# Mixture of experts in a two-layer decoder step: 64-row tiles in two weight lanes, ordered by expert size, with indirect weight loads

## The chip, the cores and the metric

The kernel runs as one program on one core of a Trainium2 chip. The metric is the device time of one execution in microseconds (us), lower is better. All data are float32.

## The reference

One inference step of a decoder with two layers (a gated linear attention layer, then a differential attention layer over a shared key and value cache). It takes a prompt of 512 tokens and 8 samples of one token each, 520 tokens in all, with a model width of 1024. Each layer ends with a mixture of experts: 16 experts in 4 groups, of which a token uses two of the same group.

```python
def moe_ffn(xm, w_router, b_router, w_gate, w_up, w_down):
    ...
    probs = jax.nn.softmax((xt @ w_router + b_router).astype(jnp.float32), axis=-1)
    pg = probs.reshape(-1, N_GROUPS, EXPERTS_PER_GROUP)
    gscore = jnp.sum(lax.top_k(pg, TOP_K)[0], axis=-1)
    gidx = jnp.argmax(gscore, axis=-1)
    in_group = jnp.take_along_axis(pg, gidx[:, None, None], axis=1)[:, 0]
    vals, idx = lax.top_k(in_group, TOP_K)
    wts = vals / jnp.sum(vals, axis=-1, keepdims=True)
    ...
    for e in range(N_EXPERTS):
        h = jax.nn.silu(xt @ w_gate[e]) * (xt @ w_up[e])
        y = y + comb[:, e:e + 1] * (h @ w_down[e])
    return y.reshape(shp)
```

`w_gate` and `w_up` of an expert are 1024 x 512, `w_down` is 512 x 1024: three matrices of 2 MB. 520 tokens with two experts each make 1040 rows per layer. How many rows an expert gets depends on the data. For the inputs of this case it is, for experts 0 to 15:

- layer 0: 32, 28, 30, 38, 43, 145, 110, 114, 117, 40, 82, 59, 54, 23, 86, 39
- layer 1: 130, 106, 126, 6, 153, 160, 5, 9, 18, 9, 68, 43, 101, 4, 8, 93

## The kernel before

The program is a row of stages with a barrier of all engines between them: the conditioning vectors, the projections of the first layer (`stage_gla_project`), its attention (`stage_gla`), the output projection and norm, then `stage_route`, `stage_experts` and `stage_combine` for the mixture of experts, then the second layer's attention (`stage_decoder`) and again route, experts and combine.

`stage_route` (L1223) multiplies the rows by the router's matrix, picks two experts per token on VectorE (DVE), counts with TensorE (PE) how many rows each expert has and which rank a row has within its expert (`rk_mm`), and from that computes with a chain of small DVE operations (L1348, L1425 to L1504): the slot of each row (`dest`), the row of each slot (`idx`), the expert of each tile (`texp`), whether a tile has more than 64 rows (`full`), and the number of pairs of tiles. Meanwhile SP loads the weights of tiles 0 and 1.

`stage_experts` (L1507) works on tiles of 128 rows. Tile n is expert n for the first 16; tiles behind them take what an expert has above 128 rows; one expert may be split in halves so that the number of tiles is even. Layer 0 has 18 tiles, layer 1 has 20. The loop `tiles` runs every engine through the tiles in order, and tiles alternate between two sets of buffers, u = 0 and 1. For tile n:

- POOL copies a column of `idx` (L1560) and gathers up to 128 rows of x by an indirect DMA (L1563), after the x transposes of an earlier tile.
- PE transposes x (L1577, 8 instructions), ACT copies the transposes (L1653), PE computes gate and up (L1629): 16 matmuls of 512 columns in two column tiles of 64 (the trace counts 32 instructions) for the first 64 rows. If `full` says so, a branch (L1593, its value loaded at L1599) does the same for the second 64 rows.
- ACT applies silu (L1675, L1676), DVE multiplies by up (L1706).
- PE transposes h (L1586, 4), ACT copies it (L1659), PE computes down (L1611, 16 instructions for 64 rows, 32 for 128), DVE and ACT copy y (L1699, L1664, L1665), and ACT's queue stores 512 KB of y (L1668).
- SP loads gate and up for tile n once the gate/up product of tile n-2 has freed the buffer, and down of tile n-1 once the down product of tile n-3 has (`load_expert`, L1204; the DMAs are L1210). The expert's number is read into a register, and every tile loads its three matrices, 2 MB each.

On PE the order for tile n is: gate/up of n, h transposes of n-1, x transposes of n+1, down of n-1. `stage_combine` (L1713) gathers two rows of y per token (L1760) and adds them by their weights. Rows of the y store that no tile reaches are filled with finite values once: `stage_gla` does that with one DMA of 4 MB on SP (L898), behind its loads of the recurrent state (L592). `stage_gla_project` (L340) runs before it; the last things that SP issues there are loads at L192 and L380.

Of the kernel before, what the change touches and what calls it, by code (L numbers as in the profile page):

```python
# [8 lines left out]
I32 = mybir.dt.int32  # L9
# [5 lines left out]
P = 128  # L15
# [52 lines left out]
def allocate(nc, ctx):  # L68
# [26 lines left out]
    m.psd = lambda n: m.ps[n]  # L95
    m.modD = nc.dram_tensor("mod_rows", (NVEC, NS + 1, D), F32).ap()
# [243 lines left out]
def stage_gla_project(nc, ctx, m, a, ahead):  # L340
# [5 lines left out]
    sh_mm, sh_cp, sm_mm, sm_ev = (sem(n) for n in ("sh_mm", "sh_cp", "sm_mm", "sm_ev"))  # L346
# [21 lines left out]
    with nc.Block() as block:  # L368
        @block.sync
        def _(sp):  # L370
            ada_next = {2: range(0, 5), 3: range(5, 9), 4: range(9, 13), 5: range(13, 16)}
            for c in range(1, 6):
# [8 lines left out]
                if c == 1:  # L381
# [7 lines left out]
                    sp.dma_start(gn, a["gn_a"][0].partition_broadcast(P)).then_inc(gn_in, 16)  # L389

# [204 lines left out]
def stage_gla(nc, ctx, m, a, states, w_out):  # L595
# [6 lines left out]
    y_fill, eg_ok, q_zero, qk_zero, qs_ok, kr_mm, kr_ok, ks_ok, kv_mm, st_ok, so_mm, o_out = (sem(n) for n in  # L602
        ("y_fill", "eg_ok", "q_zero", "qk_zero", "qs_ok", "kr_mm", "kr_ok", "ks_ok", "kv_mm", "st_ok", "so_mm", "o_out"))
# [34 lines left out]
    with nc.Block() as block:  # L638
# [254 lines left out]
        def _(sp):  # L893

            most = 2 * MIN_PAIRS * P
            for n in range(NS // 2):
                states.load(sp, n)
            sp.dma_start(m.yD[most:SLOTS, :].rearrange("(t p) n -> p t n", p=P),  # L898
                         m.x[:, 0:1, :].to_broadcast([P, (SLOTS - most) // P, D])).then_inc(y_fill, 16)

# [15 lines left out]
            sp.wait_ge(y_fill, 16)  # L916
# [280 lines left out]
def expert_weights(nc, ctx, m, l, a):  # L1197

    return [(n, [view(m.W, (2 * j + u) * 4096, k, 4096 // k) for u in range(2)], a[f"w_exp_{n}"][l],
             [ctx.enter_context(m_semaphore(nc, f"moe{l}_{n}_in{u}")) for u in range(2)], k)  # L1200
            for j, (n, k) in enumerate((("gate", KT), ("up", KT), ("down", FF // P)))]


def load_expert(sp, m, weights, tile, u, free=None):  # L1204

    e = tile if isinstance(tile, int) else sp.value_load(m.texp[0:1, tile], min_val=0, max_val=NE - 1)
    for name, buf, source, loaded, k in weights:
        if free is not None:
            wait(sp, *free[name])
        sp.dma_start(buf[u].rearrange("p k n -> p (k n)"),  # L1210
                     source[bass.ds(e, 1)].rearrange("a (p k) n -> p (a k n)", k=k)).then_inc(loaded[u], 16)
# [11 lines left out]
def stage_route(nc, ctx, m, l, a, weights, router, ada=None):  # L1223
# [19 lines left out]
    half_of, pick, room, odd = (take(1, NE)[:, 0, :] for _ in range(4))  # L1243
    over, steps = take(NE, NTT - 1), take(1, NTT - 1)[:, 0, :]
# [5 lines left out]
    nt, start, end, zero16 = (take(1, NE)[:, 0, :] for _ in range(4))  # L1250
    tmp16 = take(1, NE)[:, 0, :]
    lim = take(1, NE)[:, 0, :]
    cmp_ = take(SLOT_TILES, NE)
    cmp2 = take(MORE, NE)
    first, far = take(1, NE)[:, 0, :], take(NTT, NE)
    tix, tef = take(1, SLOT_TILES)[:, 0, :], take(1, SLOT_TILES)[:, 0, :]

    NJ = 2 * NTT
    tok, tile0, row0 = take(1, NTT)[:, 0, :], take(1, SLOT_TILES + 1)[:, 0, :], take(1, P)[:, 0, :]
    slot, row = take(2, NTT), take(1, NJ)[:, 0, :]  # L1260
    reached, token_at, row_hot = take(NJ, SLOT_TILES + 1), take(NJ, SLOT_TILES), take(NJ, P)
    assert off[0] <= 9 * D
    with nc.Block() as block:
        @block.sync
        def _(sp):
            sp.dma_start(m.lnr[:, 0, :], a["ln_ffn_g"][l].partition_broadcast(P)).then_inc(ln_in, 16)
            sp.dma_start(m.lnr[:, 1, :], a["ln_ffn_b"][l].partition_broadcast(P)).then_inc(ln_in, 16)
            load_expert(sp, m, weights[0:1], 0, 0)
            load_expert(sp, m, weights[0:1], 1, 1)
            if ada is not None:  # L1270
                sp.wait_ge(ada.used, Ada.STEPS)
            load_expert(sp, m, weights[1:3], 0, 0)
            load_expert(sp, m, weights[1:2], 1, 1)
            sp.wait_ge(ln_in, 32)

        @block.gpsimd
        def _(g):
# [10 lines left out]
            nc.gpsimd.iota(first, pattern=[[P, NE]], base=0, channel_multiplier=0, allow_small_or_imprecise_dtypes=True).then_inc(tab, 1)  # L1288
            nc.gpsimd.iota(tix, pattern=[[1, SLOT_TILES]], base=0, channel_multiplier=0,
                           allow_small_or_imprecise_dtypes=True).then_inc(tab, 1)  # L1290
            nc.gpsimd.iota(tok, pattern=[[P, NTT]], base=0, channel_multiplier=1, allow_small_or_imprecise_dtypes=True).then_inc(tab, 1)
            nc.gpsimd.iota(tile0, pattern=[[P, SLOT_TILES + 1]], base=0, channel_multiplier=0,
                           allow_small_or_imprecise_dtypes=True).then_inc(tab, 1)
            nc.gpsimd.iota(row0, pattern=[[1, P]], base=-P, channel_multiplier=0, allow_small_or_imprecise_dtypes=True).then_inc(tab, 1)
            nc.gpsimd.iota(steps, pattern=[[P, NTT - 1]], base=P, channel_multiplier=0, allow_small_or_imprecise_dtypes=True).then_inc(tab, 1)
# [5 lines left out]
        def _(pe):  # L1301
# [42 lines left out]
        def _(v):  # L1344
# [15 lines left out]
            V.memset(zero16, 1.0)  # L1360
# [31 lines left out]
            def first_of(onehot, score, best, weights, n):  # L1392
# [30 lines left out]
            tt(over, m.ps[5][:, 0:NE].unsqueeze(2).to_broadcast([P, NE, NTT - 1]), steps.unsqueeze(1).to_broadcast([P, NE, NTT - 1]),  # L1423
               ALU.is_gt)
            V.tensor_reduce(out=nt, in_=over, axis=AX.X, op=ALU.add)  # L1425
            V.scalar_tensor_tensor(out=half_of, in0=m.ps[5][:, 0:NE], scalar=0.5 * P, in1=over[:, :, 0], op0=ALU.is_gt, op1=ALU.subtract)
            v.drain()
            V.tensor_tensor_scan(end, zero16, nt, 0.0, ALU.mult, ALU.add)
            v.drain()
            V.tensor_scalar(odd[:, 1:1 + MORE // 2], tix[:, 1:MORE:2], end[:, NE - 1:NE], None, ALU.is_equal)  # L1430
            V.tensor_tensor_scan(room, zero16, half_of, 0.0, ALU.mult, ALU.add)
            v.drain()
            V.tensor_reduce(out=odd[:, 0:1], in_=odd[:, 1:1 + MORE // 2], axis=AX.X, op=ALU.add)
            V.scalar_tensor_tensor(out=pick, in0=room, scalar=1.0, in1=half_of, op0=ALU.is_equal, op1=ALU.mult)
            v.drain()
            V.tensor_scalar(pick, pick, odd[:, 0:1], None, ALU.mult)
            v.drain()
            tt(nt, nt, pick, ALU.add)
            V.tensor_tensor_scan(end, zero16, nt, 0.0, ALU.mult, ALU.add)
            V.tensor_scalar(room, pick, -0.5 * P, float(P), ALU.mult, ALU.add)  # L1440
            v.drain()
            tt(start, end, nt, ALU.subtract)

            V.tensor_tensor(far, m.ps[3][:, 0:NTT * NE].rearrange("p (i e) -> p i e", e=NE),
                            room.unsqueeze(1).to_broadcast([P, NTT, NE]), ALU.is_ge)
            V.scalar_tensor_tensor(out=lim, in0=start, scalar=float(P), in1=first, op0=ALU.mult, op1=ALU.subtract)
            v.drain()
            V.tensor_tensor(lim, lim, room, ALU.subtract)
            v.drain()
            V.tensor_scalar(lim, lim, float(NE * P), None, ALU.add)  # L1450
            V.tensor_tensor(RK, m.ps[3][:, 0:NTT * NE].rearrange("p (i e) -> p i e", e=NE),
                            first.unsqueeze(1).to_broadcast([P, NTT, NE]), ALU.add)
            v.drain()
            tt(far, far, lim.unsqueeze(1).to_broadcast([P, NTT, NE]), ALU.mult)
            tt(RK, RK, far, ALU.add)

# [1193 lines left out]
```

## Time and profile before

| | |
|---|---|
| three executions, median (lowest to highest) | 1887.97 us (1885.96 to 1888.25) |
| span of the profiled execution | 1878.7 us |
| what the median has more than that span | 9.3 us |
| PE busy / share of the span | 1551.5 us / 83% |
| DVE, ACT, POOL busy | 679.1, 404.9, 352.2 us |
| DMA | 551.63 MB, mean 294 GB/s |

The span is the time between the first and the last instruction that the profiler recorded. The profiled execution has no time of its own besides it; the difference to the median of the plain executions is what lies around the span (and what profiling itself does). Engines are PE (TensorE), PEld (its weight loads), DVE (VectorE), ACT (ScalarE), POOL (GpSimd) and SP (SyncE, which only issues DMAs here); "q" behind a name means that engine's queue or sequencer. A line such as L1629 is a line of the kernel. A stage is read from its own window, since a share over the whole span mixes stages with different limits.

### The profile page before, as it was taken

The numbers are of one execution on the slowest core, as the hardware profiler recorded it, in microseconds if no ns is written. First come the engines' busy times: TensorE is split into PE (matmuls) and PEld (weight loads), VectorE is DVE, ScalarE is ACT, GpSimd is POOL, SyncE is SP. The second block draws the span as 40 slices with busy tenths as digits, with TensorE's granted clock in tenths as the row PEclk, the third lists the DMA queues.
The fourth block names the chain that finished last, engine by engine and source line by source line (L and its number), as shares of the span: only waits on it lengthen the run. The fifth ranks groups of instructions, "written<-read, shape, count | busy, mean of one in ns | idle before, by whom it ended". The sixth has DMA issues, their size and how long they took to land. (4 is left out here: it accounts for less than half of the span.)

```text
span 1878.7 us, 21805 instructions
## 1 busy us (share of the span) xinstructions
PE 1551.5 (83%) x7246; PEld 676.2 (36%) x7247; DVE 679.1 (36%) x1228; ACT 404.9 (22%) x914; POOL 352.2 (19%) x277
## 2 busy tenths in 40 slices
PE   5999996597689998956999987887495599989965
PEld 2333344443333333313443334444142233333321
DVE  1001118475300000046945448886175300000006
ACT  1001015221121212212121113444321021222220
POOL 0000001000100000021745469872000100000001
PEclk8999997698799999977999998889697699999996
DMA  8564605726699999796889999997504499999963
GB/s 320 199 269 163 271 2 190 240 109 240 251 425 426 392 378 417 319 344 230 310 297 364 398 353 409 367 351 302 197 23 154 168 425 381 418 419 398 429 263 134
DMA packets 119419, 551.63 MB, mean 294 GB/s; under 512 B 16453, under 2 KB 37814, under 8 KB 97307
## 3 DMA queue, kind: packets, MB, share of 16 engines
q1 hardware_dynamic: 94962, 492.46, 66.4%
q10 hardware_dynamic: 15424, 37.28, 5.4%
q0 software_dynamic: 8944, 20.76, 3.2%
q8 instruction: 49, 0.80, 0.2%
q14 instruction: 40, 0.33, 0.0%
HBM read 521.82 MB, written 40.03 MB: 299 GB/s over the span
## 5 line engine op out<-in xcount | busy, mean ns | idle before, releaser
L1629 PE MATMUL ps<-arena_w,arena_r 128*64 128x512 f32 x1600 | 364.4, 612 | 27.1 <-issue 22.2
L1629 PEld LDWEIGHTS ps<-arena_w,arena_r 128*64 128x64 f32 x1600 | 121.1, 141 | 263.6 <-issue 257.4
L1611 PE MATMUL ps<-arena_w,arena_r 128*64 128x512 f32 x800 | 183.4, 606 | 19.2 <-ACT arena_r L1659 19.2
L1706 DVE TENSOR_TENSOR arena_r<-arena_r,ps 128x512 f32<-128x512 f32 x38 | 26.2, 688 | 419.9 <-ACT arena_r L1676 419.9
L2036 POOL TENSOR_TENSOR arena_w<-arena_w,arena_r 128x1024 f32<-128x1024 f32 x55 | 129.5, 2360 | 84.7 <-DMA arena_w<-in_cache_k_dram 84.3
L2036 POOL TENSOR_TENSOR arena_r<-arena_r 128x1024 f32<-128x1024 f32 x56 | 134.0, 2398 | 44.5 <-DMA arena_r<-in_cache_k_dram 44.3
L2089 PE MATMUL ps<-arena_w,xt 128*128 128x512 f32 x256 | 114.9, 606 | 1.3 <-ACT xt L2265 1.3
L450 PE MATMUL ps<-arena_w,xt 128*128 128x512 f32 x256 | 113.0, 597 | 1.0 <-DVE arena_w L533 0.6
L1098 PE MATMUL ps<-arena_w,xt 128*128 128x512 f32 x256 | 111.4, 593 | 0.0
L1560 POOL COPY small<-idx 128x1 int32 (+1 forms) x38 | 7.0, 183 | 510.4 <-PE ps L1577 459.3
L1611 PEld LDWEIGHTS ps<-arena_w,arena_r 128*64 128x64 f32 x800 | 55.3, 139 | 121.0 <-issue 99.2
L1675 ACT ACTIVATE arena_r<-ps 64x512 f32<-64x512 f32 x38 | 22.4, 588 | 339.2 <-PE ps L1629 339.2
L1699 DVE COPY arena_r<-ps 128x512 f32<-128x512 f32 x38 | 26.3, 692 | 188.5 <-PE ps L1611 188.5
L2431 DVE TENSOR_REDUCE arena_r<-arena_w 128x16 f32<-128x1024 f32 x64 | 76.1, 1212 | 36.0 <-POOL arena_w L2036 36.0
L2431 DVE TENSOR_REDUCE arena_r<-arena_r 128x16 f32<-128x1024 f32 x64 | 76.0, 1211 | 15.0 <-POOL arena_r L2036 14.8
L1739 PE MATMUL ps<-arena_r,xt 128*128 128x512 f32 (+1 forms) x80 | 46.6, 740 | 41.8 <-DMA arena_r<-y_rows,dest 30.2
L450 PEld LDWEIGHTS ps<-arena_w,xt 128*128 128x128 f32 x256 | 47.6, 190 | 65.7 <-issue 64.9
L2104 PE MATMUL ps<-arena_m,arena_r 128*16 128x512 f32 x480 | 64.6, 660 | 7.7 <-DMA arena_m<-in_cache_v_dram 7.7
L2089 PEld LDWEIGHTS ps<-arena_w,xt 128*128 128x128 f32 x256 | 48.7, 194 | 59.8 <-issue 58.2
L1098 PEld LDWEIGHTS ps<-arena_w,xt 128*128 128x128 f32 x256 | 48.0, 190 | 59.1 <-issue 59.1
L415 PE MATMUL ps<-xt,arena_w 128*128 128x512 f32 x128 | 59.7, 621 | 4.0 <-PEq L249 3.7
L1278 POOL MEMSET arena_r<- 128x128 f32 x2 | 0.4, 204 | 304.3 <-POOLq L951 304.3
(393 smaller groups left out, 1941.9 us busy)
## 6 DMA issues: line engine op xcount, KB each, us to landing
arena_w<-in_w_exp_gate_dram SPq DMA_DIRECT2D x38, 2048.0 KB, 13.7
arena_w<-in_w_exp_up_dram SPq DMA_DIRECT2D x38, 2048.0 KB, 17.3
arena_w<-in_w_exp_down_dram SPq DMA_DIRECT2D x38, 2048.0 KB, 16.7
arena_m<-in_cache_v_dram SPq DMA_DIRECT2D x120, 512.0 KB, 7.1
arena_w<-in_cache_k_dram SPq DMA_DIRECT2D x64, 512.0 KB, 8.2
arena_r<-in_cache_k_dram SPq DMA_DIRECT2D x64, 512.0 KB, 7.0
arena_w<-in_w_ada_dram SPq DMA_DIRECT2D x12, 2048.0 KB, 14.5
arena_m<-in_w_ada_dram SPq DMA_DIRECT2D x12, 2048.0 KB, 9.2
```

The source lines that it names most:

```text
L415: last = nc.tensor.matmul(m.ps[n % 2][:, :], w, m.xt[:, k, 0:SEQ], start=(k == 0), stop=(k == KT - 1))
L450: last = nc.tensor.matmul(m.ps[4 + n % 4][:, :], m.xt[:, k, i * P:(i + 1) * P], m.wr[c % 2][:, k, :], start=(k == 0), stop=(k == KT - 1))
L1098: last = nc.tensor.matmul(m.ps[(4 if n % 2 else 6) + c][0:r, :], m.xt[:, k, i * P:i * P + r], w.of(k, c), start=(k == 0), stop=(k == KT - 1))
L1611: last = nc.tensor.matmul(psy[c][at:at + 64, :], ht[u][:, k, 64 * (1 - a):64 * (2 - a)], wd[u][:, k, c * 512:(c + 1) * 512], start=(k == 0 ...
L1629: last = nc.tensor.matmul(ps[at:at + 64, :], xgt[u][:, k, 64 * a:64 * (a + 1)], w[u][:, k, :], start=(k == 0), stop=(k == KT - 1), tile_po ...
L1699: V.tensor_copy(ys[u][:, 0:512], psy[0][:, :]).then_inc(y_v, 1)
L1706: V.tensor_tensor(hs[u], es[u], psu[:, :], ALU.mult).then_inc(h_ok, 1)
L1739: last = nc.tensor.matmul(y_ps[i % 2][n][0:r, :], dg[c][i][0:r, 0:r], y[i % 2][c][0:r, n * 512:(n + 1) * 512], start=(c == 0), stop=(c == 1))
L2036: G.tensor_tensor(kp[n % RING], kp[n % RING], qb[b % 2], ALU.mult).then_inc(pp_ok, 1)
L2089: last = nc.tensor.matmul(bank[:, :], m.xt[:, k, i * P:(i + 1) * P], dec.both[c % 4 // 2][:, k, :], start=(k == 0), stop=(k == KT - 1))
L2104: last = nc.tensor.matmul(PSO[n][32 * g:32 * g + C, :], PR[b % 2][:, GRP * q + g, :], value_at(GRP * v + g)[:, n * 512:(n + 1) * 512], sta ...
L2431: V.tensor_reduce(out=S[b % 2][:, j, :], in_=kp[n % RING].rearrange("p (c d) -> p c d", d=DHB), axis=AX.X, op=ALU.add).then_inc(ks_ok, 1)
```

## The change

The mixture of experts is organized anew.

- **Tiles** have 64 rows (`TR`). Two of them, one in lane 0 (rows 0 to 63 of a pair) and one in lane 1 (rows 64 to 127), make a pair; each lane has one buffer for each of the three matrices. The pair shares one gather of x, one set of x transposes, one of h transposes.
- **Order.** The experts are ranked by their number of rows on the chip (a 16 x 16 comparison). Expert 0 is forced to the head of lane 0, expert 1 to that of lane 1. Even ranks go to lane 0 in falling order, odd ranks to lane 1 in rising order. The tiles of an expert follow each other in its lane. For the rows above that makes 12 pairs in layer 0 and 14 in layer 1. The lanes (expert: rows of its tiles):
  - layer 0, lane 0: 0: 32; 8: 64, 53; 6: 64, 46; 10: 64, 18; 12: 54; 9: 40; 3: 38; 13: 23; one empty tile. Lane 1: 1: 28; 2: 30; 15: 39; 4: 43; 11: 59; 14: 64, 22; 7: 64, 50; 5: 64, 64, 17.
  - layer 1, lane 0: 0: 64, 64, 2; 4: 64, 64, 25; 12: 64, 37; 10: 64, 4; 8: 18; 7: 9; 3: 6; 13: 4. Lane 1: 1: 64, 42; 6: 5; 14: 8; 9: 9; 11: 43; 15: 64, 29; 2: 64, 62; 5: 64, 64, 32; one empty tile.
- **Weights** of later tiles are loaded by POOL with indirect DMAs of 128 rows of 16 KB. The row numbers are computed on the chip; where a tile continues the expert of the tile before it, they lie out of bounds and the DMA moves nothing. Only the first tile of each lane is loaded by SP, at the end of the route stage.
- **Short arm.** A value per tile chooses between two code arms for each product: above 32 rows two column tiles of 64 rows with 512 columns, otherwise four column tiles of 32 with 256 columns each (gate/up; the moving operand takes 2 of every 4 columns) or with half of the sum each (down), and DVE adds the two halves (`y_join`).
- **Order of PE** for pair i: gate/up of lane 0, down of pair i-1 in lane 0, gate/up of lane 1, x transposes of pair i+1, down of pair i-1 in lane 1, h transposes of pair i.
- **Stores of y**: 64 rows as two DMAs of 512 columns per tile, on SP, behind ACT's copy and `y_join`.
- **Ahead of the loop** POOL makes three index tables, and DVE computes from them which tiles take which arm (`full_ok`) and which rows each load takes (`col_ok`): about eight operations on 128 x 832 or 128 x 52 elements. PE waits for `full_ok` ahead of the first product.
- **Routing**: the DVE chain in `stage_route` has other operations, for ranks, lanes and starts.
- **The y fill** grows to 8 MB and moves from `stage_gla` to the end of SP's program in `stage_gla_project`, with a wait for it there.

```diff
-    return [(n, [view(m.W, (2 * j + u) * 4096, k, 4096 // k) for u in range(2)], a[f"w_exp_{n}"][l],
...
+             a[f"w_exp_{n}"].rearrange("l e (p k) n -> (l e p) (k n)", k=k))
...
@@ stage_gla_project, sync engine @@
+            least = MIN_PAIRS * P
+            sp.dma_start(m.yD[least:SLOTS, :].rearrange("(t p) n -> p t n", p=P),
+                         m.x[:, 0:1, :].to_broadcast([P, (SLOTS - least) // P, D])).then_inc(y_fill, 16)
+            sp.wait_ge(y_fill, 16)
...
@@ stage_route, vector engine, behind the counts @@
+            V.scalar_tensor_tensor(out=key, in0=count, scalar=float(NE), in1=bias, op0=ALU.mult, op1=ALU.add)
...
+            V.tensor_tensor(larger, along(key), across(key), ALU.is_gt)
...
+            V.tensor_reduce(out=rank_of, in_=larger, axis=AX.X, op=ALU.add)
...
+            V.scalar_tensor_tensor(out=key, in0=lane, scalar=-100.0, in1=rank_of, op0=ALU.mult, op1=ALU.add)
...
@@ stage_experts, gpsimd @@
+            def load(which, nexts, at, i, u):
+                nc.gpsimd.tensor_copy(at[u], col[:, bass.ds(i + u * COLS, 1)])
+                g.drain()
+                for (_, buf, _, _, _, rows), landed in zip(which, nexts):
+                    g.indirect_dma_start(out=buf[u].rearrange("p k n -> p (k n)"), out_offset=None, in_=rows,
+                                         in_offset=bass.IndirectOffsetOnAxis(ap=at[u], axis=0),
+                                         bounds_check=DEPTH * NE * P - 1, oob_is_err=False).then_inc(landed[u], 16)
+
+            def step(i, t):
+                g.wait_ge(gu_mm, 2 * i + 1)
+                load(weights[0:2], (wg_next, wu_next), gi, i + 1, 0)
+                if t != 0:
+                    g.wait_ge(d_mm, 2 * i - 1)
+                    load(weights[2:3], (wd_next,), di, i, 0)
+                g.wait_ge(x_tr, i + 2)
+                gather(i + 2)
+                g.wait_ge(gu_mm, 2 * i + 2)
+                load(weights[0:2], (wg_next, wu_next), gi, i + 1, 1)
+                if t != 0:
+                    g.wait_ge(d_mm, 2 * i)
+                    load(weights[2:3], (wd_next,), di, i, 1)
...
@@ stage_experts, tensor engine @@
+            def by_size(i, u, done, whole, half):
+
+                full = pe.value_load(m.full[0:1, bass.ds(i + u * COLS, 1)], min_val=0, max_val=1)
                 with pe.If_ne(full.val, 0):
-                    product(1).then_inc(done, 1)
+                    whole().then_inc(done, 1)
                 with pe.Else():
-                    pe.nop().then_inc(done, 1)
+                    half().then_inc(done, 1)
...
+                def half():
+                    for k in range(KT):
+                        for j in range(4):
+                            w = (wg, wu)[j // 2][u][:, k, :].rearrange("p (a b) -> p a b", b=FT)
+                            out = psg[u][QR * j:QR * (j + 1), :].rearrange("t (a b) -> t a b", b=FT)
+                            last = nc.tensor.matmul(out[:, :, 0:2], xgt[:, k, TR * u:TR * u + QR], w[:, :, j % 2 * 2:j % 2 * 2 + 2],
+                                                    start=(k == 0), stop=(k == KT - 1), tile_position=(0, QR * j))
...
+            def step(i, t):
+                gate_up(i, 0, t == 0)
                 if t != 0:
...
+                    down(i - 1, 0, t == 1)
+                gate_up(i, 1, t == 0)
+                x_transpose(i + 1, False)
                 if t != 0:
...
+                    down(i - 1, 1, t == 1)
+                h_transpose(i, t == 0)
+
             pe.wait_ge(zeroed, 1)
...
+            x_transpose(0, True)
+            pe.wait_ge(full_ok, 1)
+            pairs = loop(pe, step)
...
@@ stage_experts, vector engine @@
+            def y_join(i, u):
+                V.tensor_copy(sf[u], small[:, bass.ds(i + u * COLS, 1)])
+                v.drain()
+                v.wait_ge(y_s, 2 * i + u + 1)
+                for c in range(2):
+                    r, over = slice(TR * c, TR * c + QR), slice(TR * c + QR, TR * (c + 1))
+                    last = V.scalar_tensor_tensor(out=ys[u][r, :], in0=psy[u][over, :], scalar=sf[u][over, :], in1=ys[u][r, :],
+                                                  op0=ALU.mult, op1=ALU.add)
+                last.then_inc(y_v, 1)
...
+            V.tensor_tensor(begun, at, each(code), ALU.is_ge)
+            V.tensor_tensor(within, at, each(full_to), ALU.is_lt)
+            v.drain()
+            V.tensor_tensor(begun, begun, within, ALU.mult)
...
+            v.drain().then_inc(full_ok, 1)
```

## Rows read from the trace of the kernel before

**Rows 1.** Busy windows, expert stages: span, engines (PE to POOL), PEclk, DMA share, GB/s.

```profile
486.00:804.00 318.00, 282.98 (x1320) 109.61 (x1320) 26.31 (x40) 71.79 (x128) 21.75 (x36) 0.95 0.89 367
...
1475.00:1829.00 354.00, 322.66 (x1536) 123.67 (x1536) 28.88 (x44) 79.74 (x142) 23.83 (x39) 0.97 0.89 368
```

**Rows 2.** The waits: engine line waited for: total us, times, longest.

```profile
ACT arena_r L1675 <- PE ps L1629: 339.2, 38, 19.8
```

**Rows 3.** The waits of SP's DMA queue, same columns.

```profile
SPq L1210 <- PE ps L1629: 323.9, 34, 24.2
```

**Rows 4.** PE in time: start, length (us), line, operands, idle before.

```profile
711.47 7.04 PE L1629 MATMUL ps<-arena_w,arena_r 128*64 128x512 f32 x32
718.44 0.75 PE L1586 MATMUL ps<-ident,arena_r 128*128 128x128 f32 x4
719.02 1.06 PE L1577 MATMUL ps<-ident,arena_r 128*128 128x128 f32 x8
720.41 3.65 PE L1611 MATMUL ps<-arena_w,arena_r 128*64 128x512 f32 x16 [0.32 <-ACT arena_r L1659]
728.07 16.49 PE L1629 MATMUL ps<-arena_w,arena_r 128*64 128x512 f32 x64 [4.00 <-issue]
```

**Rows 5.** Busy windows at the late product of the group above.

```profile
726.40:733.20 6.80, 5.13 (x12) 1.64 (x14) 0.00 (x0) 0.00 (x0) 0.00 (x0) 0.50 1.01 424
733.20:790.00 56.80, 54.41 (x268) 20.93 (x266) 4.83 (x7) 13.48 (x24) 1.20 (x2) 1.00 0.94 383
```

**Rows 6.** The costliest groups: out<-in xcount | busy, mean ns | idle before.

```profile
L1629 PE MATMUL ps<-arena_w,arena_r 128*64 128x512 f32 x1600 | 364.4, 612 | 27.1 <-issue 22.2
```

**Rows 7.** PE in order of time, in the first layer's attention.

```profile
314.94 3.63 PE L865 MATMUL ps<-arena_m,arena_w 128*8 128x256 f32 x64
```

**Rows 8.** POOL in order of time: one gather of x.

```profile
544.64 0.18 POOL L1560 COPY small<-idx 128x1 int32 x1 [13.79 <-PE ps L1577]
545.72 1.01 POOL L1563 DMA_INDIRECT arena_r<-xm_rows,small  x1 [0.90 <-issue]
```

**Rows 9.** Line L1563, the x gathers: ns min/median/max, landing.

```profile
L1563 POOL DMA_INDIRECT arena_r<-xm_rows,small x38: 1004/1014/1239, 487.2 to 1767.7; - x38
...
DMA to landing us min/median/max: 3.4/10.9/12.6
```

**Rows 10.** Line L1760, the gathers of y rows.

```profile
L1760 POOL DMA_INDIRECT arena_r<-y_rows,dest x20: 852/942/1950, 804.5 to 1855.2; - x20
```

**Rows 11.** Line L1599, the value load on PE's queue.

```profile
L1599 PEldq FUSED_REGOPS  x110: 37/151/156, 492.3 to 1813.2; - x110
L1599 PEldq TENSOR_LOAD <-full x76: 297/303/695, 491.9 to 1812.9; - x76
```

**Rows 12.** Line L1593, the branch on PE's queue.

```profile
L1593 PEldq COMPARE_BRANCH  x100: 66/200/352, 498.5 to 1818.9; - x100
```

**Rows 13.** PE in order of time: the first product of layer 0.

```profile
493.99 8.91 PE L1629 MATMUL ps<-arena_w,arena_r 128*64 128x512 f32 x32 [1.16 <-ACT arena_r L1653]
```

**Rows 14.** The costliest groups again: a DVE copy of 512 columns.

```profile
L1699 DVE COPY arena_r<-ps 128x512 f32<-128x512 f32 x38 | 26.3, 692 | 188.5 <-PE ps L1611 188.5
```

**Rows 15.** DVE in order of time: the first instruction of combine.

```profile
803.88 0.06 DVE L1766 MEMSET small<- 128x1 f32 x1 [3.95 <-PEq L1543]
```

**Rows 16.** DVE in order of time, route of layer 1: chain's ends.

```profile
1460.16 0.23 DVE L1348 TENSOR_TENSOR arena_r<-ps,arena_r 128x64 f32<-128x64 f32 x1 [1.55 <-PE ps L1324]
...
1466.03 0.41 DVE L1348 TENSOR_TENSOR arena_r<-arena_r 128x250 f32<-128x250 f32 x1
```

**Rows 17.** SP in order of time, from the projection stage's end.

```profile
217.30 0.55 SPq L380 DMA_DIRECT2D arena_w<-in_w_in_a_dram  x1
284.28 6.07 SPq L592 DMA_DIRECT2D arena_m<-in_state_gla_dram  x4
```

**Rows 18.** DMA issues: out<-in xcount, KB each, median us to landing.

```profile
y_rows<-x_res SPq DMA_DIRECT2D x1, 4096.0 KB, 19.7
```

**Rows 19.** DMA queues: packets, MB, share of 16 engines.

```profile
q0 software_dynamic: 8944, 20.76, 3.2%
```

More of the change, by code:

```diff
@@ L1441, in _ @@
+            V.tensor_reduce(out=tiles[:, 1:2], in_=start, axis=AX.X, op=ALU.add)
+            V.tensor_reduce(out=both_lanes, in_=nt, axis=AX.X, op=ALU.add)
+            V.tensor_reduce(out=passed, in_=whole, axis=AX.X, op=ALU.add)
             v.drain()
[L1442 to L1446, printed above, removed]
+            V.tensor_tensor(larger, along(key), across(key), ALU.is_lt)
@@ L1526, in stage_experts @@
[L1526 to L1540 removed]
+    FT, HW = FF // P, FF // 2
@@ L1640, in _, with x_copy @@
             pe.wait_ge(zeroed, 1)
-            x_transpose(0, 0, True)
-            pairs = tiles(pe, step)
-            full = is_full(bass.ds(2 * pairs - 1, 1))
-            h_transpose(1, 2 * pairs - 1)
-            down(1, 2 * pairs - 1, 16 * pairs, full)
+            x_transpose(0, True)
+            pe.wait_ge(full_ok, 1)
+            pairs = loop(pe, step)
+            for u in range(2):
+                down(pairs - 1, u, False)
         @block.scalar
         def _(s):
-            def x_copy(u, n):
-                s.wait_ge(x_tr, n + 1)
-                wait(s, gu_mm, 2 * n - 2)
+            def x_copy(i, first):
+                s.wait_ge(x_tr, i + 1)
+                if not first:
+                    s.wait_ge(gu_mm, 2 * i)
@@ L1688, in _ @@
+                h_copy(i, t == 0)
+            x_copy(0, True)
+            pairs = loop(s, step)
+            for u in range(2):
+                y_keep(pairs - 1, u, False)
         @block.vector
@@ new lines, in _ @@
+            V.tensor_tensor(within, at, each(code), ALU.is_equal)
+            v.drain()
+            V.tensor_copy(m.full[0:1, :], fullf[0:1, :])
+            V.tensor_scalar(small, fullf, -1.0, 1.0, ALU.mult, ALU.add)
+            V.tensor_tensor(within, within, each(ew), ALU.mult)
+            v.drain().then_inc(full_ok, 1)
+            V.tensor_reduce(out=lanes(fullf), in_=within, axis=AX.X, op=ALU.add)
+            v.drain()
+            V.tensor_scalar(col, fullf, prow, None, ALU.add).then_inc(col_ok, 1)
@@ L1713, in stage_combine @@
+            pairs = loop(v, step)
+            for u in range(2):
+                y_join(pairs - 1, u)
 def stage_combine(nc, ctx, m, l, a, stores=None, ada_groups=(), vectors=(), dec=None):
```

452 lines of the change are left out of this document (236 added, 216 removed).

## The prediction

> **What bounds the kernel now.** I read the stages first (the busy windows), then the waits, then TensorE's own order in time. The two expert stages are the two windows of [rows 1]: 318.0 and 354.0 us, with PE busy for 282.98 and 322.66 us, so the array works for nine tenths of them; the DMA engines are 0.89 busy at the same time and carry 367 GB/s, that is 412 GB/s when all are busy. One expert is 6.29 MB, 15.2 us of that wire: 10.2 for gate and up, 5.1 for down. ACT's longest wait is for the gate/up product [rows 2], and the loads on SP wait for the same product [rows 3]: a buffer comes free late, then the wire runs. So array and wire take turns at being last. TensorE's order [rows 4] gives the prices of the array: gate/up of 64 rows 7.04 us (6.9 to the next start), of 128 rows twice that, 13.9, down of 64 rows 3.65 (3.5 net), h transposes 0.6, x transposes 1.0, 0.3 of gap ahead of a down product. The last row there shows what a late load costs: 4.00 us of idle, then 16.49 us where 13.9 is normal. In those first 6.80 us the granted clock was 0.50 (1.2 GHz), behind them 1.00 (2.4 GHz) [rows 5]; the excess is 2.6.
>
> **The work after.** The router of the reference, worked through for its own inputs, gives the rows of each expert; 38 tiles and 50 products of 64 rows (1600 instructions of 32 each, [rows 6]) follow from it for the kernel before, as the trace has them. After: layer 0 has 12 pairs (16 tiles above 32 rows, 8 of 32 or fewer), layer 1 has 14 pairs (15 and 13). Both load 14 experts on the way, where 16 and 18 tile loads stood. In each layer one tile of the short ones is empty. Of the 11 steps from pair to pair in layer 0, 5 bring new weights to both lanes, 4 to one, 2 to none; of 13 in layer 1, 4, 6 and 3.
>
> **Prices not in the trace.** The short gate/up arm is 64 matmuls four wide over 256 columns. The nearest row is the 3.63 us of 64 such matmuls, 57 ns each [rows 7]; ends 3.5 (half of 7.04) and 7.0 (nothing won). I take 3.6, and 1.75 for the short down product. An expert load by indirect DMA: the x gather takes 0.18 for its copy, 0.90 to the issue, 1.01 for the issue [rows 8]; it lands after 3.4 at best [rows 9], of which 1.3 is wire. So a load costs 1.1 + 2.1 + wire. Rows four times as long are not in the trace; between 8 rows and 128 the issue hardly differs (0.852 to 0.942, at most 1.950, [rows 10]), so I take 1.01, with 0.85 and 4 times 1.01 as ends. A value load and branch behind a late wait cost 0.30 + 0.15 + 0.20 = 0.65, with their gaps 0.8 [rows 11, 12]; ends 0 and 1.0.
>
> **One step.** Array: gate/up and down of both lanes, transposes: 6.9 + 3.5 + 6.9 + 1.0 + 3.5 + 0.6 = 22.4 with full tiles. Lane 0 new: its load starts after its gate/up product and needs 1.1 + 2.1 + 10.2 + 0.8 = 14.2; 15.5 of array lie beside it, so it is hidden while that cover is full; with short tiles it is not. Lane 1 new: POOL has the x gather ahead of the load in its queue, and that waits for the x transposes: 1.0 + 2.4 + 14.2 = 17.6 against 15.5, so 2.1 is exposed: 24.5 with a full product, 21.2 with a short one. Both new: the wire is continuous, 1.1 + 2.1 + 10.2 + 5.1 + 10.2 + 0.8 = 29.5 from one gate/up end in lane 0 to the lane 1 product, less the 3.5 of the down product between: 26.0. x gather and y stores (0.5 MB each per pair) share that wire: 2.5 more, 28.5 (ends 26.0 and 30.5). POOL takes its waits in order (lane 0's gate/up, its down, the x gather, lane 1's gate/up, its down), so a late down product of lane 0 would hold the gather, and that lane 1's load; on the array it comes ahead of lane 1's gate/up product and the x transposes, which end 6.9 + 1.0 later, so it holds nothing. Lane 1's down weights then hold the wire for 8.6 us of the next step; if that step loads lane 0, it lands 5.4 later.
>
> Going through the pairs by these prices: layer 0, both new 5 x 28.5 = 142.5; one new 24.5 + 24.5 in lane 1, and in lane 0 behind a step with both new 14.2 + 5.4 and a full or a short product, 26.5 + 23.2, together 98.7; none 2 x 19.1 (3.5 + 6.9 + 1.0 + 3.5 + 0.6 and a short product of 3.6) = 38.2. Layer 1: both new 4 x 28.5 = 114; one new 21.2 + 21.2 + 24.5 in lane 1, 23.2 and twice 14.2 + 3.6 = 17.8 in lane 0, together 125.7; none 15.4 (first step, no down products yet), 20.7 and 17.4 (with one and three short products), together 53.5.
>
> **Head, tail, clock.** The first product starts 8.0 us after the stage begins [rows 13]; it now waits for some six DVE operations on 128 x 832 elements, about 1.0 each from 0.692 for 512 [rows 14], of which 2.8 stick out: 10.8. The first product itself comes off idle, 8.91 instead of 7.04 [rows 13], so 8.9 in layer 1 and 5.4 for the short one in layer 0. Tail: the rest of the last pair, 14.2 and 12.5; then the store and the block's end, 4.6 today (DVE's last copy, 0.69, and 3.95 of idle ahead of combine at 803.88, [rows 14, 15]), plus 1.6 for joining two halves (a small copy, ACT's copy and two DVE operations in line where two engines copied side by side): 6.2. Late loads let the clock fall: 7 and 5 waits of 4 us or more, 1.8 each (the excess of 2.6 above for a product twice as long, 8.91 against 7.04 for one), half of it beside the next load: 6.3 and 4.5 (ends 0 and 31 for both).
> Layer 0: 10.8 + 5.4 + 142.5 + 98.7 + 38.2 + 20.4 + 6.3 = 322.3, today 318.0: +4.3. Layer 1: 10.8 + 8.9 + 114 + 125.7 + 53.5 + 18.7 + 4.5 = 336.1, today 354.0: -17.9.
>
> **The other edits.** Routing: the chain from the ranks' product to the row of slots is 5.87 us of DVE now [rows 16]; about 27 operations of 0.17 to 0.41 in its place give 8.9, less 0.6 on the shorter tail behind it: +2.4 per layer, +4.8 (ends 0 and 10). The y fill doubles to 8 MB and moves to SP's last place in the projection stage: SP issues its last load there at 217.30 and has nothing until the next stage's at 284.28 [rows 17]; the 4 MB fill took 19.7 us to land [rows 18], so 8 MB take 39 at most beside products that end the stage, with 28 us to spare. If that cover went, 39 would be the worst. Taken from the state loads' stage, where it is issued behind them and waited for last, it frees nothing. y stores move from ACT to SP, which has nothing else left to do: nothing. Weight loads leave SP for POOL: counted above. Three index tables are made on POOL behind the first gather and beside its landing of 3.4 us [rows 9], and the second gather, which they delay, is needed a product later: nothing, at most the 2.8 of the head again. Two arms for every product make PE's code longer; no wait of the trace is put down to its fetching: nothing, at worst one branch of 0.65 a step, 16.
>
> Sum: +4.3 - 17.9 + 4.8 = -8.8 on the profiled execution's span of 1878.7 us. The median of the three runs, 1887.97, is 9.3 above that span; I take those 9.3 as unchanged: 1869.9 + 9.3, **1879**.
>
> **Rivals.** (a) *More is hidden*: x and y slip into gaps of the wire (9 x 2.5 = 22), no clock loss (11), no lane-1 wait (5 x 2.1 = 10): about 1836. For it: the wire has a tenth free [rows 1]; against it: one buffer per lane, so every load waits for a product. (b) *Costs cancel*, 1884 to 1892: the steps with both new at 29 to 30 (nine of them, 0.5 to 1.5 more each): the wire never catches up. (c) *POOL becomes the bound, the other side*: seven indirect DMAs and five copies a step, some 14 us by [rows 8] today, in order, with waits between. Each new lane has two issues on its chain; 19 steps load. At 1.2 us an issue the gain is gone, at 2.0 it is 19 x 2 x 1.0 = 38: 1917. For it: rows of 16 KB not seen yet, one issue of 1.95 [rows 10]; against it: 1004 to 1239 ns in 38 gathers [rows 9]. (d) *Strided moving operands don't stream at the price of* [rows 7]: 21 short tiles x 3.3 = 69 us of array, half on the path: 1914. (e) *The skip doesn't skip*: every step loads both lanes, 15 further loads and more, above 1950; against it the software queue's 20.76 MB [rows 19]: 38 gathers of 128 rows and 20 of y would be 30 MB, the valid rows of both are 17.
>
> By the Trainium skill (DMA: Bandwidth & Descriptors, SWDGE vs HWDGE vs iDMA) descriptor rings are SBUF state that GpSimd writes and that DVE's 2-port mode locks it out of, so issues would stretch beside DVE work; an estimate from 26.31 us of DVE in the stage [rows 1], twice that after, is 0.2 us an issue, 8 us, and the sum 1887. The gathers' 1239 ns at most [rows 9] shows hardly any of it.
> The Trainium skill (TensorE: Matmul & The Clock Gate, "Wait — 56ns, not 53.3ns?") gives about 62 ns of sequencer per matmul when hardware decode is off, 3.97 us for 64 of them; [rows 7] shows 57 ns, 3.63 us. By the page the sum would be 21 x 0.34 = 7 us of array more, half of it on the path.
>
> **Chances.** Forecast 0.40 (own range 1850 to 1884); (a) 0.12; (b) 0.16; (c) 0.21; (d) 0.09; (e) 0.02. Faster by over 0.2% (3.8 us, about what a measurement of this kernel can tell) 0.52, same 0.16, slower 0.32. The range takes (a) in at 1836 and (c), (d) up to 1915: 1835 to 1915.
>
> **What would show it.** Right: stages near 322 and 336 us; both-new steps at 28 to 29 us; short products at 3.6; POOL issues near 1.0; first product about 11 us in. Wrong: issues of 1.3 us or more on POOL, or steps without loads above 23 us, or short products of 5 and more; then (c) or (d) decides. Stages below 300 would mean (a).

## The result, and the profile after

The changed kernel takes 2291.27 us (median of 4; 2282.11 to 2298.47) where the kernel before takes 1888.11 us: a ratio of 1.212, 95% interval 1.208 to 1.217. It is 403 us slower; the forecast was 9 us faster, with 1915 as the upper end of the range.

The busy windows by stage show where. Columns are as in [rows 1]; the second and the fourth line are the expert stages.

```profile
0.00:491.00 491.00, 395.33 (x1848) 184.16 (x1849) 169.59 (x370) 86.15 (x170) 10.67 (x35) 0.89 0.56 213
491.00:997.60 506.60, 283.43 (x1560) 108.67 (x1560) 65.69 (x112) 50.43 (x87) 96.82 (x147) 0.78 0.55 199
997.60:1684.50 686.90, 540.05 (x2502) 257.99 (x2502) 426.33 (x721) 161.86 (x460) 286.25 (x160) 0.84 0.77 288
1684.50:2245.00 560.50, 317.25 (x1938) 121.75 (x1938) 75.16 (x127) 58.45 (x101) 112.79 (x171) 0.76 0.50 182
```

506.6 and 560.5 us stand against 318.0 and 354.0 in [rows 1]: 395 of the 417 us by which the two profiled executions differ (spans of 2296.0 and 1878.7). PE is busy about as long as before although the stage is far longer, its clock has fallen to 0.78 and 0.76, and the DMA engines, 0.89 busy before, stand at 0.55 and 0.50. So neither the array nor the wire is last. The waits name the engine (total us, times, longest):

```profile
DVE arena_r L1761 <- ACT arena_r L1725: 688.7, 52, 24.2
POOL arena_w L1578 <- issue: 626.7, 147, 13.8
ACT arena_r L1725 <- PE ps L1654: 501.9, 31, 25.1
PEld ps L1654 <- issue: 423.3, 465, 18.0
...
PE ps L1654 <- issue: 250.6, 24, 17.2
...
POOL arena_r L1571 <- issue: 132.7, 28, 10.7
```

POOL stands idle for 626.7 us ahead of its indirect weight loads (L1578) and for 132.7 us ahead of the x gathers (L1571), and no other engine releases it ("issue"). In order of time on POOL, in layer 0, the lane 1 half of one step of the loop and the lane 0 half of the next:

```profile
561.59 0.19 POOL L1575 COPY small<-xt 128x1 int32<-128x1 int32 x1
565.78 1.01 POOL L1578 DMA_INDIRECT arena_w<-in_w_exp_gate_dram,small  x1 [4.00 <-issue]
567.10 0.99 POOL L1578 DMA_INDIRECT arena_w<-in_w_exp_up_dram,small  x1 [0.31 <-issue]
568.10 0.20 POOL L1575 COPY small<-xt 128x1 int32<-128x1 int32 x1
580.84 1.01 POOL L1578 DMA_INDIRECT arena_w<-in_w_exp_down_dram,small  x1 [12.55 <-issue]
581.87 0.19 POOL L1575 COPY small<-xt 128x1 int32 x1
590.80 1.01 POOL L1578 DMA_INDIRECT arena_w<-in_w_exp_gate_dram,small  x1 [8.75 <-issue]
592.12 0.99 POOL L1578 DMA_INDIRECT arena_w<-in_w_exp_up_dram,small  x1 [0.30 <-issue]
593.12 0.19 POOL L1575 COPY small<-xt 128x1 int32 x1
606.23 1.01 POOL L1578 DMA_INDIRECT arena_w<-in_w_exp_down_dram,small  x1 [12.91 <-issue]
```

Each DMA issue takes 1.0 us, as the x gathers did [rows 8]. The copies of the indices start at once, so the semaphores that POOL waits on have come long before. But behind each copy the next DMA starts late: 4.00 us behind an x gather, 8.75 behind 2 MB, 12.55 and 12.91 behind 4 MB issued just before; the second DMA of a pair (up behind gate), which has no copy between, follows after 0.30. Between copy and DMA stands one instruction that the trace has no row for: `g.drain()`. [rows 8] shows the same place with 0.90.

What the drain waits for can be read from the landings. The view of DMAs, asked for the first six DMAs above one by one (the last number is us from issue to landing):

```profile
arena_r<-xm_rows,small POOLq DMA_INDIRECT x1, 4.4
arena_w<-in_w_exp_gate_dram,small POOLq DMA_INDIRECT x1, 8.8
arena_w<-in_w_exp_up_dram,small POOLq DMA_INDIRECT x1, 12.8
arena_w<-in_w_exp_down_dram,small POOLq DMA_INDIRECT x1, 9.1
arena_w<-in_w_exp_gate_dram,small POOLq DMA_INDIRECT x1, 9.0
arena_w<-in_w_exp_up_dram,small POOLq DMA_INDIRECT x1, 13.2
```

So the x gather landed at 564.97, and the next DMA starts 0.81 us later; up landed at 579.90 (0.94), down at 589.94 (0.86), the second up at 605.32 (0.91). The drains of both stages stand in 130 such places. In 121 of them an earlier DMA of POOL's was still on its way when the copy was done, and the DMA behind the drain starts 0.79 to 1.20 us behind the last landing; in the other 9 nothing was, and it starts 0.89 to 1.00 us behind the copy.

### The profile page after: what moved, and what is told of

The parts are those of the page before. It is cut to its first block and busy times, and to the rows that moved or that the text cites. A ratio compares the mean times of both kernels' runs of the same rounds, so it can differ in the third digit from the quotient of the medians.

```text
span 2296.0 us, 23818 instructions
## 1 busy us (share of the span) xinstructions
PE 1561.4 (68%) x7886; PEld 681.2 (30%) x7887; DVE 769.7 (34%) x1374; ACT 362.5 (16%) x834; POOL 517.7 (23%) x523
## 3 DMA queue, kind: packets, MB, share of 16 engines
q0 software_dynamic: 29680, 196.96, 23.2%
## 5 line engine op out<-in xcount | busy, mean ns | idle before, releaser
L1654 PE MATMUL ps<-arena_w,arena_r 128*64 128x512 f32 x992 | 268.7, 703 | 253.5 <-issue 250.6
L1761 DVE TENSOR_TENSOR arena_r<-arena_r,ps 64x512 f32<-64x512 f32 x52 | 35.9, 690 | 688.7 <-ACT arena_r L1725 688.7
L1654 PEld LDWEIGHTS ps<-arena_w,arena_r 128*64 128x64 f32 x992 | 89.2, 162 | 423.5 <-issue 423.3
L1663 PE MATMUL ps<-arena_w,arena_r 128*32 128x256 f32 x1344 | 109.5, 494 | 107.3 <-issue 105.2
L1769 DVE SCALAR_TENSOR_TENSOR arena_r<-ps,small,arena_r 32x512 f32<-32x512 f32 x104 | 78.0, 750 | 224.9 <-ACT arena_r L1731 224.2
L1725 ACT ACTIVATE arena_r<-ps 64x512 f32<-64x512 f32 x52 | 30.6, 588 | 705.1 <-PE ps L1654 501.9
L1680 PE MATMUL ps<-arena_w,arena_r 128*64 128x512 f32 x496 | 122.8, 641 | 26.5 <-issue 17.3
L1578 POOL DMA_INDIRECT arena_w<-in_w_exp_down_dram,small x48 | 48.7, 1015 | 375.9 <-issue 374.1
L1578 POOL DMA_INDIRECT arena_w<-in_w_exp_gate_dram,small x52 | 52.8, 1015 | 238.0 <-issue 238.0
L1663 PEld LDWEIGHTS ps<-arena_w,arena_r 128*32 128x32 f32 x1344 | 50.7, 137 | 168.9 <-issue 153.2
L1688 PE MATMUL ps<-arena_w,arena_r 128*32 128x512 f32 x336 | 52.2, 744 | 47.1 <-issue 45.2
L457 PEld LDWEIGHTS ps<-arena_w,xt 128*128 128x128 f32 x256 | 47.9, 191 | 66.0 <-issue 65.2
```

The costliest lines, as they stand in the source:

```text
L457: last = nc.tensor.matmul(m.ps[4 + n % 4][:, :], m.xt[:, k, i * P:(i + 1) * P], m.wr[c % 2][:, k, :], start=(k == 0), stop=(k == KT - 1))
L1578: g.indirect_dma_start(out=buf[u].rearrange("p k n -> p (k n)"), out_offset=None, in_=rows, in_offset=bass.IndirectOffsetOnAxis(ap=at[u], ...
L1654: last = nc.tensor.matmul(psg[u][TR * j:TR * (j + 1), :], xgt[:, k, lane_rows[u]], w[u][:, k, :], start=(k == 0), stop=(k == KT - 1), tile ...
L1663: last = nc.tensor.matmul(out[:, :, 0:2], xgt[:, k, TR * u:TR * u + QR], w[:, :, j % 2 * 2:j % 2 * 2 + 2], start=(k == 0), stop=(k == KT - ...
L1680: last = nc.tensor.matmul(psy[u][TR * c:TR * (c + 1), :], ht[:, k, lane_rows[u]], wd[u][:, k, c * 512:(c + 1) * 512], start=(k == 0), stop ...
L1688: last = nc.tensor.matmul(psy[u][QR * j:QR * (j + 1), :], ht[:, b, TR * u + QR * s:TR * u + QR * (s + 1)], wd[u][:, 2 * s + b, c * 512:(c ...
```

## The experiments

**Without the drain.** The drain only has to keep the DMA from reading an index that the copy has not written yet. A semaphore does that too (the small addition carries the wait):

```diff
-                nc.gpsimd.tensor_copy(at[u], col[:, bass.ds(i + u * COLS, 1)])
-                g.drain()
+                nc.gpsimd.tensor_copy(at[u], col[:, bass.ds(i + u * COLS, 1)]).then_inc(ready[u], 1)
+                g.wait_ge(ready[u], i)
+                nc.gpsimd.tensor_tensor(spare, code[:, 0:1], code[:, 0:1], ALU.add)
```

and the same in `gather`. Expected:

> The drain that POOL executes between copying an index column and issuing the indirect DMA is replaced by a semaphore that the copy raises. Theory D (the drain waits until every DMA that POOL issued earlier has landed, so its loads run one pair at a time and also wait for the skipped ones): idle time of POOL ahead of its indirect weight loads falls from 626.7 us to below 150, the two expert stages from 507 and 560 us to 320 to 350 each, the whole to 1880 to 1930 us. Rival Q (the software queue has room for two 2 MB loads only, and a third issue waits for room): the 12 to 13 us of idle behind each pair of gate and up loads stay, the whole stays above 2200. Rival W (indirect loads are slow on the wire itself): POOL's idle time goes but the product's wait on PE stays, landing grows beyond 25 us in the median, the whole stays above 2150.

Measured: 1932.44 us, ratio to the kernel before 1.023 (1.018 to 1.028). 359 of the 403 us are gone, though the total lies just above the 1930 that D allowed, and the second stage above its 350. POOL's idle time ahead of its loads falls from 626.7 to 69.0 us. On POOL the loads now follow each other, each 0.53 us after its addition:

```profile
545.38 0.20 POOL L1578 COPY small<-xt 128x1 int32<-128x1 int32 x1
545.67 0.19 POOL L1580 TENSOR_TENSOR small<-xt 128x1 f32<-128x1 f32 x1
546.38 1.03 POOL L1582 DMA_INDIRECT arena_w<-in_w_exp_gate_dram,small  x1 [0.53 <-issue]
547.72 0.99 POOL L1582 DMA_INDIRECT arena_w<-in_w_exp_up_dram,small  x1 [0.30 <-issue]
548.72 0.19 POOL L1578 COPY small<-xt 128x1 int32<-128x1 int32 x1
549.00 0.19 POOL L1580 TENSOR_TENSOR small<-xt 128x1 f32<-128x1 f32 x1
549.71 1.03 POOL L1582 DMA_INDIRECT arena_w<-in_w_exp_down_dram,small  x1 [0.53 <-issue]
```

These are lane 1's gate and up for pair 2 (expert 15) and its down for pair 1 (expert 2), all new: three loads of 2 MB issued within 4.4 us. The queue has room for more than two, and rival Q is out. W is out as well: it wanted landings of over 25 us in the median, and they take 10.7 (22.7 at most); the stages are 330.9 and 379.0 us (first index copy on POOL to the first instruction of combine), at 305 and 269 GB/s. The loads are the changed kernel's own; only the wait between them went.

**The drain back at one place.** In e1_no_drain the drain stands again ahead of the x gather, and only there:

```diff
-                nc.gpsimd.tensor_copy(xi, m.idx[:, bass.ds(i, 1)]).then_inc(xi_ok, 1)
-                g.wait_ge(xi_ok, i + 1)
-                nc.gpsimd.tensor_tensor(spare, code[:, 0:1], code[:, 0:1], ALU.add)
+                nc.gpsimd.tensor_copy(xi, m.idx[:, bass.ds(i, 1)])
+                g.drain()
```

> As e1_no_drain, but with the drain back ahead of the x gather alone, one of five in a step. Theory D (a drain lasts until POOL's earlier DMAs have landed): the idle time ahead of the gather is 5 us and more in the steps in which lane 0 got new weights just before, 2.5 or less in the others; lane 1's load starts that much later; the whole is 50 to 130 us above e1_no_drain. Rival F (a drain costs a fixed time, whatever is under way): the same idle time in every step, and about a fifth of the 359 us between the changed kernel and e1_no_drain, 70 us. Idle times tell the two apart.

Measured: 2006.91 us, ratio 1.063 (1.058 to 1.068), 74 us above e1_no_drain. That total fits both theories; the idle times of the gathers (last column) fit only one:

```profile
522.74 1.02 POOL L1573 DMA_INDIRECT arena_r<-xm_rows,small  x1 [10.85 <-issue]
...
550.70 1.02 POOL L1573 DMA_INDIRECT arena_r<-xm_rows,small  x1 [1.33 <-issue]
...
584.51 1.02 POOL L1573 DMA_INDIRECT arena_r<-xm_rows,small  x1 [6.27 <-issue]
...
613.85 1.01 POOL L1573 DMA_INDIRECT arena_r<-xm_rows,small  x1 [1.44 <-issue]
```

These are the gathers of the first four steps. Lane 0 changes its expert in the steps to pairs 1 and 3 and keeps it in those to 2 and 4; the drain waits 10.85 and 6.27 us in the former, 1.33 and 1.44 in the latter. So it is not a fixed price. But the change of lane 0 alone doesn't tell its length: of the 14 steps of both layers with new weights in lane 0, six stay under the 5 us expected (2.74 to 4.85), and of the 12 others three exceed 2.5 (3.16, 6.09 and 7.04). The landings do. In 17 of these 26 steps a landing later than the copy is on record, and the gather starts 1.07 to 1.17 us behind it; in eight every landing on record lies before the end of the copy, and the wait is 1.10 to 1.44 (in the two shown, a down matrix of 2 MB landed at 546.51 and 612.09, ahead of copies at 549.19 and 612.24). The landing that the first one, 10.85, waited for is not in the view. That is theory D: the drain lasts until the DMAs that POOL issued before have landed.

**The same drain in the kernel before.** The replacement at the one gather per tile of the kernel before:

```diff
-                nc.gpsimd.tensor_copy(ixc[u], m.idx[:, bass.ds(2 * i + u, 1)])
-                g.drain()
+                nc.gpsimd.tensor_copy(ixc[u], m.idx[:, bass.ds(2 * i + u, 1)]).then_inc(ix_ok, 1)
+                g.wait_ge(ix_ok, 2 * i + u + 1)
+                nc.gpsimd.tensor_tensor(spare, m.wts[:, 0, 0:1], m.wts[:, 0, 0:1], ALU.add)
```

> The kernel before with the same replacement of the drain ahead of its x gather. Theory D: its gathers (512 KB, one a tile, 12 us and more apart) have mostly landed when the next drain comes, so the drain cost nothing there: within 0.3% of the kernel before, the idle time ahead of the gathers falls from 51 to 20 to 30 us. Rival F: some 1 us a tile that lies on no path: the same time too, so the time alone can't tell them; what would speak against both is a gain of more than 0.5%.

Measured: 1892.51 us, ratio 1.002 (1.000 to 1.004). The idle time ahead of the gathers (L1563, L1564 here) falls from 51.3 to 19.4 us, and the time doesn't fall. A drain that waits for one gather, with a product's time to spare, was hidden there. That it waits could have been read from the kernel before, at the head of its first expert stage, in the same view as [rows 8]:

```profile
487.24 1.24 POOL L1563 DMA_INDIRECT arena_r<-xm_rows,small  x1 [0.98 <-issue]
488.50 0.19 POOL L1560 COPY small<-idx 128x1 int32<-128x1 int32 x1
491.62 1.02 POOL L1563 DMA_INDIRECT arena_r<-xm_rows,small  x1 [2.93 <-issue]
```

The second gather's copy is done at 488.69, and the DMA starts 2.93 later instead of 0.90 to 0.98: the first gather, issued at 487.24, was still on its way (PE starts on it at 490.88).

**The order on POOL.** From e1_no_drain, the x gather is moved behind lane 1's gate and up loads:

```diff
-                g.wait_ge(x_tr, i + 2)
-                gather(i + 2)
                 g.wait_ge(gu_mm, 2 * i + 2)
                 load(weights[0:2], (wg_next, wu_next), gi, gi_ok, i + 1, 1)
+                g.wait_ge(x_tr, i + 2)
+                gather(i + 2)
```

> As e1_no_drain, and the x gather is moved on POOL behind lane 1's gate and up loads. Theory D with the prediction's step prices: lane 1's load starts up to 2.4 us plus the x transposes earlier wherever lane 1 is new, in 9 + 5 steps; 10 to 30 us below e1_no_drain. If the loads' own issue or the wire is last in those steps, no more than 5 us. Rivals Q and W: within 10 us of e1_no_drain.

Measured: 1904.49 us, ratio 1.007 (1.005 to 1.010): 28 us less, at the upper end of D's 10 to 30. Lane 1's load no longer stands behind the gather's wait for the x transposes.

**The short arm.** From e1_no_drain, every tile with rows takes the 64-row arm, since half a tile is no longer taken off the rows at which the full arm ends:

```diff
-            V.tensor_scalar(key, code, -float(QR) / TR, None, ALU.add)
+            V.tensor_scalar(key, code, 0.0, None, ALU.add)
```

> As e1_no_drain, but every tile that has rows takes the full arm, the short arm only the two empty tiles. By the prediction's prices 19 tiles cost 3.3 us more of array in gate/up and 1.75 more in down, 96 us of array, about half beside late loads: 30 to 60 us above e1_no_drain. If the short arm's strided columns stream at half rate (the prediction's rival d), within 15 us of it. If loads are last nearly everywhere (W), within 10 us.

Measured: 1976.66 us, ratio 1.045 (1.040 to 1.051): 44 us more, as priced. In e2_gather_last, a short gate/up product undisturbed and a full one (PE in order of time):

```profile
653.75 3.84 PE L1667 MATMUL ps<-arena_w,arena_r 128*32 128x256 f32 x64
...
687.14 7.09 PE L1658 MATMUL ps<-arena_w,arena_r 128*64 128x512 f32 x32
```

Taking two of every four columns doesn't slow the stream: 60 ns a matmul, close to the 57 of [rows 7].

**The end of the stage.** e1_no_drain and e2_gather_last have a new gap: the waits give 22.3 us in both layers together between the last joining of halves and combine, where the kernel with drains has 7.6 and the kernel before 7.9. The experiment adds one line to e2_gather_last:

```diff
             pairs = loop(g, step)
+            g.drain()
             g.wait_ge(x_in, 16 * pairs + 32)
```

> As e2_gather_last, plus one drain on POOL straight behind its last load of the stage, ahead of its waits for the y stores. In e2_gather_last 10.6 and 11.7 us of DVE's idle time stand between the last joining of halves and the combine stage, 3.8 with the drains in the loop. Theory E (POOL's last drain, at the block's end, has to work off all DMAs that no drain has followed, some 90 a layer): that work now lies beside the last down products and y stores, the two gaps fall to 4 to 6 us, the whole by 9 to 15 us, to about 1890 to 1896. Rival (the gap is the y stores' landing or the added semaphores): the gaps stay above 9 us, the whole within 4 us of e2_gather_last.

Measured: 1886.43 us, ratio 1.000 (0.998 to 1.002): 18 us less, more than the 9 to 15 expected. The gaps give 14.9 of them; the rest isn't explained. The same wait before and behind the edit, first e2_gather_last, then e4_drain_at_end:

```profile
DVE small L1865 <- PEq L1546: 22.3, 2, 11.7
```

```profile
DVE small L1866 <- PEq L1546: 7.4, 2, 3.7
```

The work that a last drain has to do lies beside the last products now. e7_before_no_drain gives a second dose: without drains its two gaps grow from 7.9 to 10.9 us for 38 DMAs, and here from 7.6 to 22.3 for 182. That is 0.08 us for each DMA in both; these two doses are all that stands behind the figure.

**The head.** In the changed kernel SP loads lane 1's first down matrix (2 MB) at the stage's start, beside the first x gather. From e4_drain_at_end:

```diff
             _, buf, source, loaded, k, _ = weights[2]
+            sp.wait_ge(x_in, 16)
             sp.dma_start(buf[1].rearrange("p k n -> p (k n)"),
```

and `full_ok` is raised right behind the cast of `full` (two operations of 1.0 us go behind it).

> As e4_drain_at_end, plus two edits at the stage's head: PE is told of the table of arms as soon as it is written, two DVE operations of 1.0 us earlier, and SP loads lane 1's first down matrix (2 MB) only when the first x gather has landed. Theory: that load holds the wire while the gather (issued at 491.6 in layer 0) lands, which takes until 499.6 instead of some 2.4 to 3.4 us; the first product starts 3 to 4 us earlier in each layer, the whole is 5 to 8 us shorter than e4_drain_at_end. Rival (the head hangs on DVE's table operations alone): 1.5 to 2 us a layer, 3 to 4 in all. If the first steps' weight loads end last anyway: within 2 us.

Measured: 1875.88 us, ratio 0.994 (0.992 to 0.997): 0.6% faster than the kernel before. It is 10.6 us less than e4_drain_at_end, more than the 5 to 8 expected. Gather and x transposes of layer 0 in e4_drain_at_end and in e5_head (POOL and PE in order of time; the fences are two views of each):

```profile
486.31 1.25 POOL L1574 DMA_INDIRECT arena_r<-xm_rows,small  x1 [0.65 <-issue]
```

```profile
494.11 1.94 PE L1625 MATMUL ps<-ident,arena_r 128*128 128x128 f32 x8 [9.43 <-DMA arena_r<-xm_rows,small]
```

```profile
487.80 1.25 POOL L1575 DMA_INDIRECT arena_r<-xm_rows,small  x1 [0.65 <-issue]
```

```profile
491.63 1.94 PE L1626 MATMUL ps<-ident,arena_r 128*128 128x128 f32 x8 [5.45 <-DMA arena_r<-xm_rows,small]
```

7.8 us from the gather's issue to its use become 3.8. The first product starts 9.4 us after the first index copy (486.69 to 496.05) instead of 13.1 (485.20 to 498.33). The gather's landing is 4.0 us shorter by the load that waits; what `full_ok` added isn't known, since the two edits were not tried apart. The expert stages of e5_head are 309.7 us (486.69 to 796.35) and 341.4 us (1476.39 to 1817.80).

## Why the prediction was wrong

**The step that failed** is the price of a load under "Prices not in the trace": "So a load costs 1.1 + 2.1 + wire". Of the 1.1, 0.90 is the time from the index copy to the issue [rows 8]. I took it as a constant and put ends (0.85 and 4 times 1.01) on the issue alone. It is the drain, and it lasts as long as what POOL has under way: 4.0 us behind an x gather, 8.75 behind one matrix, 12.6 to 12.9 behind a pair, 1.75 behind a skipped load. With five drains a step and nearly all weights on POOL's queue, the loads of the two lanes ran one behind the other, while "One step" had them share a continuous wire. Taking the drain away gave back 359 us.

**Rival (c)** had the engine right and the reason wrong. An issue of 16 KB rows takes 0.99 to 1.04 us, as one of 4 KB rows; no weight load reached the bound it named (issues of 1.2 us and more). What it called "with waits between" was nearly the whole cost (359 of 403 us), and it had no price.

**What held.** The skip skips: the software queue moved 196.96 MB, 176 (28 loads of 6.29) above its 20.76 of [rows 19], so rival (e) is out. The short arm cost 3.84 (predicted 3.6) and 1.92 (1.75), and rival (d) is out. The y fill of 8 MB landed after 33.9 us (39 at most) behind SP's last load and cost nothing: the next stage starts on SP at 285.40, 67.0 us after that load (218.41), and 67.0 after it in [rows 17]. Routing: from the ranks' product to `idx` 14.9 us (475.99 to 490.88) against 13.5 (1460.16 to 1473.62): +1.4, where +2.4 stood.

**Mis-sized terms.** The head: 10.8 predicted, 13.2 measured (491.35 to 504.53), and the 2 MB load on SP beside the gather had no row in my sum; with it held back (and `full_ok` earlier) 9.4 are left. The x gather in lane 1's way: priced at 2.1 in five steps, worth 28 us in all; in which steps wasn't looked at. The work of the last drain had no term either: 14.7 us in the two stages of e1_no_drain. The lost clock was put at 11 us in all. In the changed kernel it stands at 0.78 and 0.76 in the two stages, in e1_no_drain at 0.88 and 0.86, and the same products keep PE busy 28 and 34 us longer (283.43 against 255.62, 317.25 against 282.83); how much of that lay on the path isn't shown. The steps of layer 0 together (first product of pair 0 to that of pair 11) take 274.7 us in e2_gather_last, 503.74 to 778.44, against 142.5 + 98.7 + 38.2 = 279.4. Those of layer 1 (first product of pair 0 to that of pair 13) take 303.7, 1504.41 to 1808.13, against 114 + 125.7 + 53.5 = 293.2. So the step prices, added up, were within 4% for loads that don't wait for each other, too high in one layer and too low in the other, and e2_gather_last already has the gather out of lane 1's way. That the forecast of 1879 is near the 1875.88 of e5_head is in part luck: e5_head has edits to the order, the last drain and the head that the forecast did not price, and its stages of 309.7 and 341.4 us stand where 322.3 and 336.1 were forecast. e1_no_drain, which lacks the drains alone, is 53 us above the forecast.

**Two other prices.** By the Trainium skill (DMA: Bandwidth & Descriptors, SWDGE vs HWDGE vs iDMA) DVE in its 2-port mode locks GpSimd out of the state in which it writes descriptors; the prediction had issues stretch beside DVE work by that. DVE was busy for 65.69 us of the first expert stage, and the 152 weight loads took 986 to 1027 ns each: the trace shows no such stretch for this mix of DVE operations. By the Trainium skill (TensorE: Matmul & The Clock Gate, "Wait — 56ns, not 53.3ns?") a matmul costs about 62 ns of sequencer when hardware decode is off. 3.84 us for 64 is 60 ns, between that and the 57 of [rows 7]; no run here shows how they were decoded.

**Left open.** The attention stage between the expert stages, whose code is unchanged, takes 501.9 us in the changed kernel's profile (1061.77 to 1563.62) and 488.9 in the kernel before (863.83 to 1352.69). The other seven profiles have 492.0 to 499.0, e7_before_no_drain 494.3 among them. These are single executions, and no run was made for the difference.

## What to carry to other kernels

A drain between two instructions of a queue that also issues DMAs can be a wait for all of them: count it as a wait of its own, with what is under way at that moment, and order a small copy ahead of its DMA by a semaphore. Where a row's idle time is called "issue", look at the longest of its kind besides the typical one, and ask what was under way then (0.9 and 2.93 in the same loop). Of a change that moves loads to another queue, first ask which of that queue's waits were free only because it carried little.

## What the runs showed that I had not expected

POOL's drain lasts until POOL's own DMAs have landed: the DMA behind it starts 0.79 to 1.20 us after the last landing (121 places of the changed kernel), so it waits 12.91 us behind a pair of 2 MB loads and 1.75 behind a skipped one. Where no drain follows the DMAs, the last one at the end of the block takes 0.08 us for each of them: 14.7 us for 182, 3.0 for 38. And an indirect load whose rows are all out of bounds still takes 1.0 us to issue and lands 2.1 us after its start (the down load at 606.23 in the changed kernel).
